# Five edits to one decoder-layer kernel: two stage edges removed, the selected branch rebuilt, queries reversed early, a bank copied in mid-logits, and an output projection of seven products

## The chip, the cores and the metric

One program on one NeuronCore of a Trainium2 chip, all of it in float32. The metric is the device time of one execution in microseconds (us), lower is better; the time of the kernel before is the median of three runs.

## The reference, cut to what matters

One layer with d_model 1024: a prompt of 1024 tokens, and 8 sample sequences of 4 new tokens each (32 rows) behind a past of 8192 tokens.

```python
def layer(x_prompt, x_sample, caches, page_table, weights):
    q, k, v, gates = split(rms_norm(x, norm_attn) @ w_in)
    a = dilated_attention(q_a, k_a, v_a)               # 8 heads: (window, dilation) (128,1), (512,4), (2048,16)
    c, p = compressed_attention(q_b, mlp(blocks of 64))# 8 query heads, 2 KV heads
    s = attention over the 16 blocks with the largest p, gathered from the paged pool
    w = attention over a window of 512
    mix = concat(a, g0 * c + g1 * s + g2 * w)          # sigmoid gates; T5 bias on every logit
    x1 = x + mix @ w_out                               # (1024 + 32) x 1024 by 1024 x 1024
    u = causal_conv3(rms_norm(x1, norm_ffn) @ w_up)    # 2 x 2816 columns
    return rms_norm(x1 + (silu(u_gate) * u_value) @ w_down, ...), new cache rows
```

## The kernel before, in words

Five functions run one after the other: `front` (the combined projection and the compression MLP), `compressed_and_dilated` (stage `cd`: the compressed and dilated attention of the sample rows, the choice of blocks, and the compressed attention of the prompt), `sample_selected` (`sb`: the selected and window branches of the samples), `prompt_attention` (`pa`: 12 pairs of prompt heads, `it`, by 8 tiles of 128 queries, which gives 96 units `u`), and `ffn`. Each has a `block` of its own: one instruction list for each engine, written out by hand, with semaphores between them. At the end of a block `Mem.end` lets GpSimd clear the stage's semaphores and every engine meets at a barrier; nothing of the next stage starts before. Each stage also allots its own PSUM tensors (eight banks of 128 x 512).

In `cd` the sample keys of four dilated tiles are transposed by TensorE (L1459), copied out by ScalarE and VectorE (L1649, L1644), and multiplied (L1478) with QX, the queries placed in a zeroed tensor: GpSimd zeroes it, VectorE places eight pieces (L1791). At its end the SP queue loads the window keys (L1427), eight tables of window bias (L125, into `sample_turned`), and stores the mixed sample rows (L1434).

In `sb`, for each of 8 sequences b and 4 chunks c, GpSimd gathers 128 keys and 128 values times 16 from the pool (L142, L2033: 1.05 MB each); TensorE transposes the keys (L2139), ScalarE and VectorE copy the banks out (L2277, L2236), TensorE forms scores; VectorE adds bias and takes the maximum; ScalarE takes one exponential of a whole row of 2052 (L2294) when c is 0 for the sequence before; then the probabilities are transposed (L2160) and multiplied with the values (L2178). Copies alternate between the two engines by the number of the bank. The window branch lies inside b = 0. The merge at the end is a chain of small steps (L2372 to L2405).

In `pa` a unit's logits go through VectorE (L1155) in chunks of at most 512 keys for two heads. TensorE's iteration s does the scores of unit s, the transposes of the probabilities of unit s-2 into three banks `psT` (L1029), and their product with the values (L1049). About a third of the banks is copied out by VectorE (L1181), the others by ScalarE (L1129). VectorE's iteration does both chunks of logits(s), the maxima, and then its copies of unit s-2:

```python
for s in range(U + 4):          # VectorE
    if s < U: logits(s)         # one or two chunks, two heads each
    if 2 <= s < U + 2: copies(s - 2)
```

Before unit 0 GpSimd reverses the first pair's queries (L1079, L1080).

In `ffn` the prompt's output projection runs by `out_tile` for 8 tiles of 128 rows: two halves of 512 columns with 8 matmuls each (L2728), VectorE adds x (L3047) to give x1, ScalarE squares and sums, VectorE and ScalarE form the norm, VectorE scales (L3055) into `xn`, TensorE transposes it (L2741), and both engines copy it out. Then follow seven products for each block of the up-projection, M1 to M7 (L2773), whose operand sums GpSimd and VectorE make (L2902 to L2907, L3071).

## Time and profile before

| | |
|---|---|
| time, median of 3 runs | 2149.1 us (2148.54 to 2150.56) |
| the profiled execution | 2152.93 us, its span 2151.2 us |
| granted TensorE clock, mean | 0.981 |
| TensorE, VectorE busy | 95%, 50% of the span |
| ScalarE, GpSimd busy | 24%, 25% |

In the rows PE is TensorE's matmul, PEld its weight load, DVE is VectorE, ACT ScalarE, POOL GpSimd, SP the sync engine; a q behind the name (PEq, SPq) is its sequencer. One 128-row matmul of 512 columns in the program is recorded as two. A program of this size runs each stage about once, so a stage's gain is read off one stretch of the timeline.

### The profile page before, as it was taken

What the parts mean: (1) busy time and instruction counts of PE and PEld (TensorE: products, weight loads), DVE (VectorE), ACT (ScalarE), POOL (GpSimd) and SP (SyncE); (2) the same over time, 40 slices, a digit from 0 to 9 for tenths busy, and PEclk for the clock granted to TensorE, in tenths of its full rate; (3) what the DMA queues carried; (4) which work ended last, traced back from release to release, by engine and by line L of the source; (5) the groups of instructions that cost most, each with busy time, mean ns of one, the idle gap of its engine ahead of it and who ended that gap; (6) DMA issues with size and microseconds to landing.
All of it is one profiled execution on the core that took longest, in us unless ns stands there. A gap on an engine that the chain in (4) does not pass through costs nothing. (4 is left out here: it accounts for less than half of the span.)

```text
span 2151.2 us, 31682 instructions
## 1 busy us (share of the span) xinstructions
PE 2051.5 (95%) x12366; PEld 1339.3 (62%) x12366; DVE 1082.9 (50%) x2484; ACT 521.6 (24%) x1106; POOL 532.7 (25%) x714
## 2 busy tenths in 40 slices
PE   6999999998977997999999999999999999999998
PEld 3445466665545665666676447888888888734443
DVE  5035455411525455666776226767777765611452
ACT  4111011001323344766766111011111111000011
POOL 1444234202024551012222101222322222303110
PEclk9999999998999998999999999999999999999999
DMA  8477678643697996222251414666556622601100
GB/s 219 138 241 258 243 294 305 236 170 109 231 339 290 402 396 226 99 67 68 82 155 39 133 60 156 215 208 204 196 196 211 220 79 60 227 12 30 42 40 39
DMA packets 156393, 373.05 MB, mean 173 GB/s; under 512 B 36981, under 2 KB 95085, under 8 KB 138189
## 3 DMA queue, kind: packets, MB, share of 16 engines
q1 hardware_dynamic: 126580, 149.89, 22.2%
q0 software_dynamic: 25280, 149.44, 18.0%
q10 hardware_dynamic: 4384, 71.68, 9.5%
q8 instruction: 99, 1.62, 0.3%
q14 instruction: 50, 0.41, 0.1%
HBM read 343.68 MB, written 98.60 MB: 206 GB/s over the span
## 5 line engine op out<-in xcount | busy, mean ns | idle before, releaser
L2773 PE MATMUL ff_ps<-ff_hx,whole_aw 128*128 128x264 f32 x2464 | 550.5, 386 | 0.9 <-DVE ff_hx L3074 0.9
L2773 PEld LDWEIGHTS ff_ps<-ff_hx,whole_aw 128*128 128x128 f32 x2464 | 467.1, 190 | 80.8 <-issue 1.4
L802 DVE STREAM_TRANSPOSE whole_space<-whole_space 128x512 f32<-128x512 f32 x256 | 155.3, 674 | 153.7 <-PE in_psH L611 142.0
L575 PE MATMUL in_ps<-in_w,in_xT 128*128 128x512 f32 (+1 forms) x512 | 201.5, 547 | 0.0
L1155 DVE CUSTOM_DVE_ANT_0 pa_L<-pa_psS,whole_space 128x512 f32<-128x512 f32 (+3 forms) x288 | 138.9, 532 | 46.8 <-PE pa_psS L1008 45.8
L575 PEld LDWEIGHTS in_ps<-in_w,in_xT 128*128 128x128 f32 x512 | 95.0, 190 | 94.2 <-issue 87.6
L1135 ACT ACTIVATE pa_L<-pa_L,pa_nm 128x640 f32<-128x640 f32 (+3 forms) x192 | 141.9, 741 | 32.3 <-DVE pa_nm L1165 30.5
L2799 PE MATMUL ff_ps<-ff_hx,whole_space 128*128 128x512 f32 x336 | 148.0, 593 | 0.0
L700 ACT ACTIVATE in_yout<-in_ps 128x128 f32<-128x128 f32 (+5 forms) x88 | 41.0, 479 | 378.8 <-PE in_ps L575 199.6
L3155 DVE SCALAR_TENSOR_TENSOR whole_space<-whole_space,ff_kept 128x1024 f32<-128x1024 f32 x88 | 123.3, 1401 | 3.1
L611 PE MATMUL in_psH<-whole_space 128*64 128x256 f32 (+1 forms) x1152 | 121.6, 364 | 0.0
L1008 PE MATMUL pa_psS<-whole_space,pa_qT 64*128 64x512 f32 (+3 forms) x576 | 115.3, 506 | 5.6 <-POOL pa_qT L1079 5.6
L589 PE MATMUL in_ps<-in_xT,in_w 128*128 128x352 f32 x384 | 117.6, 463 | 0.0
L2799 PEld LDWEIGHTS ff_ps<-ff_hx,whole_space 128*128 128x128 f32 x336 | 63.6, 190 | 80.6 <-issue 80.6
L2996 ACT ACTIVATE whole_space<-whole_space 128x1056 f32<-128x1056 f32 x22 | 23.8, 1084 | 368.6 <-DVE whole_space L3157 368.6
L1029 PE MATMUL pa_psT<-whole_ident,pa_L 128*128 128x128 f32 x816 | 111.9, 281 | 0.2 <-DVE pa_PT L1181 0.2
L1029 PEld LDWEIGHTS pa_psT<-whole_ident,pa_L 128*128 128x128 f32 x816 | 87.3, 141 | 39.5 <-issue 18.3
L2728 PE MATMUL ff_ps<-whole_space 128*128 128x512 f32 x256 | 111.2, 593 | 0.0
L1049 PE MATMUL pa_psO<-pa_PT,whole_space 128*64 128x128 f32 x1632 | 110.3, 279 | 0.9 <-DVE pa_tmp L1193 0.5
L1129 ACT ACTIVATE pa_PT<-pa_psT 128x512 f32<-128x512 f32 (+2 forms) x182 | 91.9, 541 | 75.9 <-PE pa_psT L1029 74.3
L611 PEld LDWEIGHTS in_psH<-whole_space 128*64 128x64 f32 x1152 | 74.9, 137 | 47.1 <-issue 13.0
L589 PEld LDWEIGHTS in_ps<-in_xT,in_w 128*128 128x128 f32 x384 | 71.8, 190 | 42.2 <-issue 3.8
(411 smaller groups left out, 2579.9 us busy)
## 6 DMA issues: line engine op xcount, KB each, us to landing
out_new_a_k_s<-in_cache_a_k ACTq DMA_DIRECT2D x8, 4088.0 KB
out_new_a_v_s<-in_cache_a_v ACTq DMA_DIRECT2D x8, 4088.0 KB
whole_aw<-in_w_up SPq DMA_DIRECT2D x44, 512.0 KB
in_w<-in_w_in SPq DMA_DIRECT2D x5, 2048.0 KB
whole_space<-in_cache_a_k SPq DMA_DIRECT2D x8, 1024.0 KB
whole_space<-in_cache_a_v SPq DMA_DIRECT2D x8, 1024.0 KB
ff_hx<-in_w_down SPq DMA_DIRECT2D x14, 512.0 KB, 4.7
whole_space<-in_x_prompt SPq DMA_DIRECT2D x13, 512.0 KB, 4.0
```

The lines of the kernel that those rows point to most:

```text
L575: mm = pe.matmul(ps[0:n, b, 0:width], xT[:, k, t * P:t * P + n], w[:, at % WBUF, k, 0:width], start=(k == 0), stop=(k == KC - 1))
L589: mm = pe.matmul(ps[:, b, 0:n], w[:, at % WBUF, k, c * P:c * P + P], xT[:, k, r0:r0 + n], start=(k == 0), stop=(k == KC - 1))
L611: mm = pe.matmul(psH[dh * HD:dh * HD + HD, r % 2, o0:o0 + n], w1[:, kv, t16, dh, :], rows[:, dh, t, :], start=(t16 == 0), stop=(t16 == 15) ...
L802: last = dve.transpose(put[:, dh, :, k * HD:k * HD + HD].rearrange("p t (g b) -> p t g b", g=2), got[:, :, :, dh, :])
L1008: pe.matmul(psS[:, c % 2, h, 0:w], qT[r, i, qt * P:qt * P + P], kT[i][r, j0 * P + k0:j0 * P + k0 + w], start=True, stop=True).then_inc(s_q ...
L1029: mm = pe.transpose(psT[:, b % 3, (x - x0) * P:(x - x0) * P + P], turned, ident[:, :])
L1135: nc.scalar.activation(x, x, ACT.Exp, bias=nm[:, s, h:h + 1], scale=1.0, accum_out=sm[:, s, h:h + 1]).then_inc(s_ex, 1)
L1155: dve.tensor_tensor_reduce(L[:, u % 3, h, 512 * x:512 * x + n], psS[:, c % 2, h, 0:n], T[it % 2][:, h, SEQ - w + 512 * x:SEQ - w + 512 * x ...
L2728: mm = pe.matmul(ps[:, j % 6, :], mixT[:, k, t * P:t * P + P], wo[:, k, half * 512:half * 512 + 512], start=(k == 0), stop=(k == KC - 1))
L2773: mm = pe.matmul(ps[:, bank_of(x, j, g), 0:H2], aw[:, j % 2, at, k, :], hx[:, bt, k, g * H2:g * H2 + H2], start=(k == 0), stop=(k == KH - 1))
L2799: mm = pe.matmul(ps[:, b, :], a[:, k, :], wd(k0 + k)[:, c0:c0 + 512], start=(k == 0), stop=(k == KD - 1))
L3155: dve.scalar_tensor_tensor(out=out[:, 0:SEQ], in0=U[:, v, k:k + SEQ], scalar=tap(k), in1=out[:, 0:SEQ], op0=ALU.mult, op1=ALU.add)
```

## The change

**Edges.** `front` and `cd` now share one block and one tensor of eight banks, and so do `sb` and `pa` (`Mem(..., within)` takes over the other's semaphores and ends nothing). Waits on `ended[...]`, the counts at which `front`'s engines are done, take the barrier's place, and `s_merged`, `s_mixc`, `s_q0`, `s_qr` do between `sb` and `pa`. GpSimd instead of VectorE places QX. **The end of `cd`.** The window bias goes to ScalarE's queue, the window keys and values are loaded with four neighbouring rows to a partition, the stores of mixc come after them and are waited for later. **The selected branch.** `by_act` names who copies which bank; the window branch comes one chunk later; the exponential is split in four, two at c = 0 and two at c = 1, and the sums are joined by one reduction. **First queries.** GpSimd reverses them at the end of `sb`, ahead of the merge. **Bank copy.** `copy_bank` stands between the two chunks of logits. **Seven products.** The output projection is one level of Strassen-Winograd: quadrants of 4 x 128 rows by 4 x 128 columns, seven products o1 to o7 of 4 tiles with 4 matmuls.

```diff
@@ class Mem
-    def __init__(self, nc, stack, stage):
-        self.nc, self.stack, self.stage, self.sems = nc, stack, stage, []
-        stack.callback(self.end)
+    def __init__(self, nc, stack, stage, within=None):
+        self.nc, self.stack, self.stage, self.sems = nc, stack, stage, within.sems if within else []
+        if within is None:
+            stack.callback(self.end)
@@ compressed_and_dilated, gpsimd
+            pool.wait_ge(*ended["copied"])
             pool.memset(QX[:, :, :, :], 0.0).then_inc(d_z, 1)
+            pool.wait_ge(d_q, 16)
+            pool.wait_ge(d_z, 1)
+            for h2 in range(2):
...
+                    pool.tensor_copy(put, got).then_inc(d_qx, 1)
@@ compressed_and_dilated, sync
+            sp.wait_ge(*ended["jobs"])
+            sp.wait_ge(*ended["copied"])
...
-             io["cache_win_k"][4 * x:4 * x + 4, :, :].rearrange("b (t p) c -> p b t c", p=P)).then_inc(pre.s_wk, 16)
+             io["cache_win_k"][4 * x:4 * x + 4, :, :].rearrange("b (p t) c -> p b t c", t=4)).then_inc(pre.s_wk, 16)
...
-            pre.load_window_bias(sp)
             pre.load_new_values(sp)
-            sp.wait_ge(s_st, 16 * QT)
@@ compressed_and_dilated, tensor
+                if n == 0 and h == 0:
+                    pe.wait_ge(*ended["half"])
...
+                        pe.wait_ge(*ended["by_act"])
+                        pe.wait_ge(*ended["by_dve"])
+                        pe.wait_ge(*ended["copied"])
                         pe.wait_ge(d_rep, 1)
                         pe.wait_ge(d_ab, 2)
                         pe.wait_ge(d_qx, 8)
@@ compressed_and_dilated, scalar
+            act.wait_ge(d_qk, 2 * NB)
+            pre.load_window_bias(act)
@@ sample_selected
+        def by_act(kind, *at):
+            if kind == "keys":
+                return at[2] == 3 if at[1] == 1 else at[2] % 2 == 0
+            if kind == "probs":
+                return at[1] in (0, 2)
+            return kind in ("window", "wprobs") and at[0] % 2 == 0
@@ sample_selected, gpsimd
+            pool.wait_ge(ops.s_q0, 16)
+            half = SEQ // 2
+            for x in range(2):
+                pool.tensor_copy(ops.q0[:, x * half:x * half + half].rearrange("p (t n) -> p t n", n=P),
+                                 backwards(ops.qL[0][:, x * half:x * half + half], half // P)).then_inc(ops.s_qr, 1)
@@ sample_selected, tensor
-                pe.wait_ge(s_ex, b + 1)
                 for c in range(NQ):
+                    pe.wait_ge(s_ex, NQ * b + c + 1)
@@ sample_selected, scalar
-                    if b >= 1 and c == 0:
+                    if b >= 1 and c in (0, 1):
                         act.wait_ge(s_nm, b)
-                        x = L[(b - 1) % 2]
-                        nc.scalar.activation(x, x, ACT.Exp, bias=nm[:, b - 1:b], scale=1.0,
-                                             accum_out=sm[:, b - 1:b]).then_inc(s_ex, 1)
+                        for i in (2 * c, 2 * c + 1):
+                            x = L[(b - 1) % 2][:, i * 512:LROW if i == 3 else i * 512 + 512]
+                            nc.scalar.activation(x, x, ACT.Exp, bias=nm[:, b - 1:b], scale=1.0,
+                                                 accum_out=sm[:, b - 1, i:i + 1]).then_inc(s_ex, 1)
@@ prompt_attention, vector: logits(u), behind the first chunk
+                    if x == 0 and between(u):
+                        copy_bank(u - 2, first_bank(u - 2))
...
+            def copy_bank(u, b):
...
+                if u >= 3:
+                    dve.wait_ge(s_wt, u - 2)
+                dve.wait_ge(s_tr, b + 1)
+                dve.tensor_copy(PT[:, u % 3, x0:x0 + w], psT[:, b % 3, 0:w]).then_inc(s_cd, 1)
@@ ffn, tensor
-            def out_tile(i):
...
+            def out_product(b, a, c):
+                for k in range(KH):
+                    mm = pe.matmul(ps[:, b % 6, :], a[:, k, :], c[:, k, :], start=(k == 0), stop=(k == KH - 1))
+                return mm
...
+                pe.wait_ge(s_ot2, 1)
+                for t in range(4):
...
+                    out_product(18 + t, A21o[t], T12o).then_inc(s_o6, 1)
+                    if t:
+                        transposes(t - 1)
+                pe.wait_ge(s_ot4, 1)
+                for t in range(4):
...
+                    out_product(22 + 2 * t, A22o[t], T4o).then_inc(s_o4, 1)
...
+                    pe.wait_ge(s_os3, t + 1)
+                    out_product(23 + 2 * t, A21o[t], T3o).then_inc(s_o7, 1)
+                    transposes(3 + t)
@@ ffn, gpsimd: the sums of the left operand, and the lower half's V
+            for t in range(4):
+                pool.tensor_tensor(A21o[t], A21o[t], A22o[t], ALU.add).then_inc(s_os1, 1)
...
+                pool.tensor_tensor(x1[5 + t][:, 0:512], x1[5 + t][:, 0:512], V[t], ALU.add).then_inc(s_bl, 1)
+                pool.tensor_tensor(x1[5 + t][:, 512:D], x1[5 + t][:, 512:D], V[t], ALU.add).then_inc(s_br, 1)
@@ ffn, vector
+                dve.tensor_tensor(V[t], ps[:, (18 + t) % 6, :], V[t], ALU.add).then_inc(s_v2, 1)
...
+                dve.tensor_tensor(x, x, V[t], ALU.add).then_inc(s_x1, 2)
+                if t == 3:
+                    dve.wait_ge(s_ot4, 1)
+                    dve.tensor_tensor(T3o, T12o, B11o, ALU.subtract).then_inc(s_ot3, 1)
```

The rows of the orders below name the line, the operation, the tensors and the output's shape; `late_bank` is the eight-bank tensor that `sb` and `pa` share. First SP's list where `cd` ends and `sb` begins, before:

```order
L1420 DMA scr_mixc<-cd_qp 128x512 x6
L1420 DMA scr_mixc<-cd_Lp 128x512 x2
L130 DMA sample_kcs<-scr_pen 128x1x1024
L1423 DMA sample_knew<-scr_s_w 32x128
L1424 DMA sample_knew<-out_new_slc_k_s 32x128
L1427 DMA whole_space<-in_cache_win_k 128x16x128 x2
L125 DMA sample_turned<-scr_tabW 16x1x516 x8
L120 DMA sample_turned<-scr_s_w 4x8x128
L120 DMA sample_turned<-out_new_slc_v_s 4x8x128
L1434 DMA scr_mixT<-cd_mixA 128x4x32
```

and SP's list at the same place after the change:

```order
L131 DMA sample_kcs<-scr_pen 128x1x1024
L1449 DMA sample_knew<-scr_s_w 32x128
L1450 DMA sample_knew<-out_new_slc_k_s 32x128
L1453 DMA whole_space<-in_cache_win_k 128x4x512 x2
L1458 DMA scr_mixc<-cd_qp 128x512 x6
L1458 DMA scr_mixc<-cd_Lp 128x512 x2
L121 DMA sample_turned<-scr_s_w 4x8x128
L121 DMA sample_turned<-out_new_slc_v_s 4x8x128
L1462 DMA scr_mixT<-cd_mixA 128x4x32
```

The eight tables (L125) are gone from this list, and the stores of mixc lie behind the window keys. Next VectorE in `pa`, a unit with two chunks of 512 keys, before (ISA is the fused add and maximum, and the read of its result):

```order
L1155 ISA pa_L,pa_mx<-pa_psS,whole_space 128x512
L1155 ISA pa_mx 128x1
L1155 ISA pa_L,pa_mx<-pa_psS,whole_space 128x512
L1155 ISA pa_mx 128x1
L1155 ISA pa_L,pa_mx<-pa_psS,whole_space 128x512
L1155 ISA pa_mx 128x1
L1155 ISA pa_L,pa_mx<-pa_psS,whole_space 128x512
L1155 ISA pa_mx 128x1
L1161 TENSOR_TENSOR pa_mm<-pa_mx 128x2
L1165 TENSOR_SCALAR pa_nm<-pa_mm 128x2
L1181 COPY pa_PT<-pa_psT 128x512
L1181 COPY pa_PT<-pa_psT 128x128
```

and the same unit on VectorE after the change:

```order
L1171 ISA pa_L,pa_mx<-late_bank,whole_space 128x512
L1171 ISA pa_mx 128x1
L1171 ISA pa_L,pa_mx<-late_bank,whole_space 128x512
L1171 ISA pa_mx 128x1
L1196 COPY pa_PT<-late_bank 128x512
L1171 ISA pa_L,pa_mx<-late_bank,whole_space 128x512
L1171 ISA pa_mx 128x1
L1171 ISA pa_L,pa_mx<-late_bank,whole_space 128x512
L1171 ISA pa_mx 128x1
L1179 TENSOR_TENSOR pa_mm<-pa_mx 128x2
L1183 TENSOR_SCALAR pa_nm<-pa_mm 128x2
L1196 COPY pa_PT<-late_bank 128x128
```

The copy of the first bank of unit u-2 has moved up by two fused operations and the two small ones; 31 units have it so. Last TensorE in the output projection, before (L2741 are the transposes of a finished tile, L2719 closes the sample rows):

```order
L2719 MATMUL ff_ps<-whole_space,ff_stack 32x512 x2
L2728 MATMUL ff_ps<-whole_space 128x512 x32
L2741 MATMUL ff_ps<-whole_ident,ff_hx 128x32 x8
L2728 MATMUL ff_ps<-whole_space 128x512 x16
L2741 MATMUL ff_ps<-whole_ident,ff_hx 128x128 x8
L2728 MATMUL ff_ps<-whole_space 128x512 x16
```

and TensorE at the same place after the change:

```order
L2805 MATMUL ff_ps<-whole_space,ff_stack 32x512 x2
L2809 MATMUL ff_ps<-whole_space 128x512 x72
L2876 MATMUL ff_ps<-whole_ident,ff_hx 128x32 x8
L2809 MATMUL ff_ps<-whole_space 128x512 x4
L2876 MATMUL ff_ps<-whole_ident,ff_hx 128x128 x8
L2809 MATMUL ff_ps<-whole_space 128x512 x4
L2876 MATMUL ff_ps<-whole_ident,ff_hx 128x128 x8
L2809 MATMUL ff_ps<-whole_space 128x512 x8
```

Before, a tile's sixteen matmuls lie between two sets of transposes; now 72 come first, then four between sets for three tiles, then eight, and the projection has 112 of them instead of 128.

## Rows read from the trace of the kernel before

**Rows 1.** Busy time and instructions of each engine, from the page's first part.
```profile
PE 2051.5 (95%) x12366; PEld 1339.3 (62%) x12366; DVE 1082.9 (50%) x2484; ACT 521.6 (24%) x1106; POOL 532.7 (25%) x714
```
**Rows 2.** TensorE's waits: waiting line, releaser, us in total, times, longest.
```profile
PE sb_psT L2139 <- ACT whole_space L2277: 14.1, 9, 4.6
PE pa_psT L1029 <- DVE pa_PT L1181: 11.8, 9, 1.4
PE sb_psT L2069 <- PEq L69: 9.4, 1, 9.4
...
PE pa_psS L1008 <- POOL pa_qT L1079: 5.6, 1, 5.6
PE cd_psT L1459 <- PEq L69: 5.4, 1, 5.4
```
**Rows 3.** Timeline from front to cd: start, duration, instructions, [idle before <-releaser].
```profile
507.93 0.54 POOL L890 DMA_DIRECT2D scr_qT<-in_yout  x1 [4.19 <-ACT in_yout L700]
...
512.58 2.89 PE L1459 MATMUL cd_psT<-whole_ident,whole_space 128*128 128x128 f32 x12 [5.44 <-PEq L69]
513.60 2.82 DVE L1791 COPY cd_QX<-sel_dq 64x32 f32<-64x32 f32 x8
523.42 1.94 PE L1478 MATMUL cd_psS<-sample_turned,cd_QX 128*32 128x512 f32 x8
...
532.25 1.06 PE L1478 MATMUL cd_psS<-sample_turned,cd_QX 128*32 128x512 f32 x8
```
**Rows 4.** Timeline where cd ends; SPq rows are DMA issues.
```profile
626.39 0.46 DVE L1808 COPY cd_mixA<-cd_psT 64x64 f32<-64x64 f32 x2 [0.75 <-PE cd_psT L1514]
626.80 6.30 SPq L125 DMA_DIRECT2D sample_turned<-scr_tabW  x8
...
634.07 0.39 SPq L1434 DMA_DIRECT2D scr_mixT<-cd_mixA  x1
```
**Rows 5.** Windows, cd's first us and two sequences of sb: engines' busy us, PEclk, DMA share, GB/s.
```profile
507.10:512.60 5.50, 0.06 (x2) 0.05 (x1) 0.02 (x1) 0.46 (x1) 0.60 (x2) 0.72 0.09 33
735.30:776.90 41.60, 37.80 (x487) 26.47 (x486) 20.17 (x44) 16.42 (x28) 25.54 (x24) 0.96 1.00 409
```
**Rows 6.** Timeline of sb: one value gather and one exponential.
```profile
690.29 0.96 POOL L2033 DMA_INDIRECT whole_space<-in_cache_slc_v,sample_idx  x1 [14.57 <-PE sb_psT L2139]
...
693.69 2.00 ACT L2294 ACTIVATE sb_work<-sb_work,sb_nm 128x2052 f32<-128x2052 f32 x1 [2.12 <-DVE sb_nm L2337]
```
**Rows 7.** Timeline from sb's last step to pa's first logits.
```profile
831.76 0.60 DVE L2405 TENSOR_TENSOR whole_space<-sample_mixB,sb_o 64x128 f32<-64x128 f32 x2
...
836.98 0.29 DVE L1155 CUSTOM_DVE_ANT_0 pa_L<-pa_psS,whole_space 128x128 f32<-128x128 f32 x1 [4.62 <-PE pa_psS L1008]
```
**Rows 8.** Timeline of one unit of pa with two chunks.
```profile
885.77 1.53 PE L1029 MATMUL pa_psT<-whole_ident,pa_L 128*128 128x128 f32 x12
...
886.38 0.69 DVE L1155 CUSTOM_DVE_ANT_0 pa_L<-pa_psS,whole_space 128x512 f32<-128x512 f32 x1
...
888.00 0.69 DVE L1181 COPY pa_PT<-pa_psT 128x512 f32<-128x512 f32 x1
...
888.74 0.33 PE L1029 MATMUL pa_psT<-whole_ident,pa_rgB 128*128 128x128 f32 x1 [1.44 <-DVE pa_PT L1181]
```
**Rows 9.** The output projection: group of its matmuls (busy us, mean ns), and its window.
```profile
L2728 PE MATMUL ff_ps<-whole_space 128*128 128x512 f32 x256 | 111.2, 593 | 0.0
```
```profile
1191.90:1314.20 122.30, 121.69 (x345) 58.76 (x345) 31.35 (x53) 17.84 (x39) 10.35 (x9) 1.00 0.23 78
```
**Rows 10.** Timeline of VectorE and GpSimd around one output tile, and at the end.
```profile
1248.78 0.69 DVE L3047 TENSOR_TENSOR ff_hx<-ff_ps,whole_space 128x512 f32<-128x512 f32 x1 [6.08 <-PE ff_ps L2728]
...
1251.31 1.28 DVE L3055 SCALAR_TENSOR_TENSOR ff_hx<-ff_hx,ff_rstd,whole_space 128x1024 f32<-128x1024 f32 x1 [0.27 <-ACT ff_rstd L2968]
...
1309.75 1.93 DVE L3055 SCALAR_TENSOR_TENSOR ff_hx<-ff_hx,ff_rstd,whole_space 128x1024 f32<-128x1024 f32 x1 [0.27 <-ACT ff_rstd L2968]
1310.68 2.13 POOL L2904 TENSOR_TENSOR whole_aw<-whole_aw 128x512 f32<-128x512 f32 x1
```

More of the change, by code:

```diff
@@ L892, in _ @@
             pool.wait_ge(s_ps, 32)
-    return total
+    return total, ended
 def backwards(x, tiles=1):
@@ L1140, in _, with first_bank, between @@
             n_mm = 0
+            def first_bank(u):
+                return bank0[u] if on_dve(bank0[u]) else None
+            def between(s):
+                return 2 <= s < U and first_bank(s - 2) is not None and chunk0[s + 1] - chunk0[s] == 2
             def logits(u):
@@ L2648, in up_weights @@
                                  wup[:, v, :, j * P:j * P + P]).then_inc(s_wu[j % 2], 16)
+            for i in range(1, NTILE):
+                sp.dma_start(x1[i], x_rows(order[i])).then_inc(s_x[1 + i // 5], 16)
             sp.wait_ge(s_cv, 1)
```

432 lines of the change are left out of this document (288 added, 144 removed).

## The prediction

> **What bounds the kernel now.** I read the page's busy times first: TensorE works 95% of the span, no other engine above 50% [rows 1]. So time is won only by fewer matmuls or by closing TensorE's waits. The list of its waits names the places [rows 2]: 5.4 us behind the barrier into `cd`, 9.4 into `sb`, 5.6 for the first queries of `pa`, 11.8 in nine waits for VectorE's bank copy, and 14.1 inside `sb` for ScalarE's key copies. The timelines around each place say what would be late next. Last, the windows show where TensorE is not the limit: two sequences of `sb` take 41.60 us with 37.80 us of TensorE work, at a DMA share of 1.00 and 409 GB/s [rows 5]. In the output projection TensorE is busy 121.69 of 122.30 us [rows 9].
>
> **The change part by part.** Gains are against the profiled execution's 2152.93 us.
>
> A, the edge into `cd`. TensorE starts at 512.58 after 5.44 us of waiting, then waits again while VectorE places QX (8 copies, 2.82 us) before its bank copies; the first scores end at 523.42 + 1.94 = 525.36 [rows 3]. The granted clock was 0.72 of full in the idle stretch before [rows 5], and the first scores took 1.94 us where later ones of the same form took 1.06 [rows 3]. After the change transposes can follow at 507.1. VectorE begins with bank copies, so what is late next is GpSimd: it issues its last DMA until 508.5 [rows 3], then zeroes and places QX. Its eight placements have no row; between VectorE's 2.82 us for all and twice that, I take 2.8, which with the zeroing puts QX near 512.5. The scores then end near 514.9: a gain of 10.5 (6 if GpSimd takes double and the barrier's waits come back in part, 11.5 if QX is never waited for). The rest of `cd` follows from TensorE, and keeps the shift.
>
> B, the edge into `sb`. `cd`'s last computing step ends at 626.39 + 0.46 = 626.85, but SP issues the eight tables for 6.30 us and its last store ends at 634.07 + 0.39 = 634.46 [rows 4]; TensorE's 9.4 us of waiting [rows 2] ends at 635.7. With the tables on ScalarE, idle there, and the stores of mixc issued while SP waits anyway, SP's last issue ends near 627.4, and the barrier needs its 1.2 us more: 7.0 (5 to 8). The tables are needed only by the window branch, which is a chunk later. The cover of their landing is the first three key chunks; were it gone, their 6.3 us would stand there.
>
> C, inside `sb`. The key copies wait behind a whole-row exponential of 2.00 us [rows 6], part of the 14.1 us [rows 2]; in four pieces, no copy waits for more than about 0.5. By TensorE's waits alone up to 11 us could come back. But the window at share 1.00 [rows 5] says that in the steady part the gathers set the pace: 16 gathers of 1.05 MB in 41.60 us are 2.6 us each, TensorE's 3.8 us of slack in it are their shadow. What can be won lies where DMA was not full: GpSimd's wait of 14.57 us for the first reused value buffer at 690.29 [rows 6], in which the gathers stand still. There the exponential's 2.00 us and the row of copies behind it go early, 3.5 us by the order; the rest of the dips I put at 3.5 more. I take 7, with 3 (the first refill alone) and 11 as ends. The two window loads have four times longer pieces, and start 7 us earlier; the one wait for them is in the 3.5.
>
> D, the edge into `pa`. The merge ends at 831.76 + 0.60 = 832.36, the first logits start at 836.98 after 4.62 us [rows 7], because SP waits for the block's start, and GpSimd reverses only then (5.6 us of TensorE [rows 2]). With q0 ready, scores of unit 0 are formed during the merge, so logits follow at once: 4.6 (3.5 to 5). GpSimd's reversal, about 1 us, is ahead of the merge where its engine has nothing to do.
>
> E, the bank copy. The first bank of u-2 is transposed by about 886.3 (12 transposes in 1.53 us from 885.77, three banks), while VectorE works the first chunk until 886.38 + 0.69 = 887.07; its copy starts only at 888.00 and TensorE waits 1.44 us for it [rows 8]. In mid-logits the copy ends at 887.8, 0.9 us before, and the second chunk's end moves from 887.7 to 888.4. TensorE's next need is then that chunk's bank, 0.7 later than now, in the next iteration. It has over 2 us of products in between. Of 11.8 us I take 10.5 (8 to 11.5).
>
> F, seven products. 16 matmuls fewer, at 2 x 111.2 / 256 = 0.87 us each [rows 9], are 13.9 us. Against them: the last tiles are now bound by a chain on VectorE, add (0.69) to scaling (1.28, ending 3.8 us after the add began) to transposes and copies [rows 10], while a tile of the sixth product gives TensorE only 4 x 0.87 + 1.0 = 4.5 us. VectorE's own work a tile there is two adds, scaling, copy and the small ones, 5.2 us or more, so TensorE waits 2 to 3 us over three tiles, and 0.6 at the end; another 1 for sums of B (128 x 2048) that VectorE holds. GpSimd's 20 additions at 1.27 us are off the path except for contention: where one lay beside the scaling, they took 2.13 and 1.93 instead of 1.27 and 1.28 [rows 10]. Three such meetings on the path cost 2. So 13.9 - 4 - 2 = about 8 (5 to 10; -1 if the next paragraph's rule holds throughout).
>
> The Trainium skill, page "SBUF — State Buffer", section "SBUF: two separate sides", says that VectorE and GpSimd share a pair of ports as an exclusive lock: a VectorE operation with two SBUF inputs and a GpSimd one that reads SBUF block each other wholly. The row pair above agrees in kind (0.65 us and 0.86 us lost at one overlap). By that rule the 20 additions of 1.27 us would all stand in VectorE's way, 25 us at the very most, and the projection could gain nothing.
>
> **Sum.** 10.5 + 7.0 + 7.0 + 4.6 + 10.5 + 8.0 = 47.6 us, so 2105.3 for a profiled execution. The profiled one of before stands 3.8 us above the median of its runs, so I predict 2101.5, say 2101. By the lower ends the gain is 30.5 (2118.6), by the upper ones 57 (2092).
>
> **Rivals.**
> 1. *The gathers hold `sb`.* For it: share 1.00 and 409 GB/s over 41.60 us [rows 5]. Everything that comes earlier on TensorE then waits for DMA. Against: the 14.57 us in which GpSimd itself stood [rows 6]. Gain without C: 2101 + 7 = 2108.
> 2. *The output projection gains nothing.* VectorE's chain and GpSimd's additions take turns; the pair at 1309.75 and 1310.68 shows it once [rows 10]. Its eight lower tiles' additions each meet a scaling. Gain without F: 2109.
> 3. *The edges don't open.* The waits on `ended` and on GpSimd's QX take the barrier's place, and `sb` still starts when SP is through (8 stores of mixc, two key loads). Half of A, B and D, 11 us, is gone: 2112. For it: GpSimd's list in `cd` begins with work that VectorE did. Against: 508.5 to 512.5 is before today's restart.
> 4. *The other side: the mid-logit copy holds VectorE.* VectorE stands in 31 units at a bank that TensorE has not transposed yet, since that needs the exponential of u-2, and the second chunk, its maxima and the next exponential all come later. If it stands x us and TensorE behind it, the time is 2101 + 10.5 + 31x, above 2149.1 from x = 1.2 on; at 1.3 it is 2152. For it: VectorE's list has no slack in such a unit. Against: the bank is there 0.8 us ahead [rows 8], so the transposes would have to come 2 us later.
>
> **Chances.** The forecast 0.50; rival 1 0.13; rival 2 0.13; rival 3 0.10; two of these together, near 2117, 0.06; rival 4 0.06; something I don't see 0.02. Within 0.2% (4.3 us, about what a measurement of this kernel can tell from no change) takes nearly an exact offset: 0.02. Slower is rival 4: 0.06. Faster 0.92. The range reaches down past the upper ends by a few us, for TensorE at full clock where it idled, to 2088, and up to two rivals together with their spread, 2123.
>
> **What the changed profile would show.** A: no wait on the sequencer near 507; transposes there, first scores before 516. B: no table DMA on SP; TensorE idle under 3 us between `cd` and `sb`. C: `sb` from its first matmul to the merge 7 us shorter; GpSimd's wait near 690 shorter by 3 or more; share still 1.00 in the steady part. D: first logits within 0.5 us of the merge's last step. E: no wait of 1.4 us for VectorE's copy, and no wait of VectorE for TensorE at the new copy. F: 112 matmuls in about 114 us in place of 122.3, with waits of 1 to 3 us for VectorE in the upper tiles. I am wrong if TensorE waits in `cd` for GpSimd's QX, if `sb` keeps its length, if VectorE stands at the mid-logit copy, or if the output projection's waits on VectorE sum to over 8 us.

## The result, and the profile after

The changed kernel takes 2128.79 us (median of 6 runs, 2126.58 to 2133.57); the kernel before took 2149.83 over all of its six runs. The ratio is 0.9902, 95% interval 0.9884 to 0.992: faster by 21 us, or 1%, where 48 us were predicted, and outside the predicted range of 2088 to 2123. The profiled execution of the changed kernel is 2126.58 us, so the two traces lie 26.4 us apart (spans 2151.2 and 2124.8). Against the traces the prediction missed 21.2 us.

The ledger cuts both traces at the same marks: the end of the last step of `cd`, the first matmul of `sb`, the end of the merge, the first logits and the end of the last product of `pa`, and then the first matmul of `ffn`, of the output projection, and of the second product of the up-projection.

| stretch | before, us | after, us | gain | predicted |
|---|---|---|---|---|
| start of the program to `cd`'s last step (A) | 626.85 | 615.02 | 11.8 | 10.5 |
| `cd`'s last step to `sb` (B) | 8.88 | 5.51 | 3.4 | 7.0 |
| `sb` to the end of the merge (C) | 196.64 | 190.82 | 5.8 | 7.0 |
| merge to first logits (D) | 4.61 | 0.03 | 4.6 | 4.6 |
| first logits to last product of `pa` (E) | 343.11 | 341.46 | 1.7 | 10.5 |
| last product to `ffn` | 1.90 | 7.20 | -5.3 | 0 |
| `ffn`'s sample rows | 9.87 | 12.39 | -2.5 | 0 |
| output projection (F) | 122.41 | 115.26 | 7.2 | 8.0 |
| the rest | 836.88 | 837.11 | -0.2 | 0 |

So most of the miss in these two traces lies in two places: the bank copy, and an edge of which the prediction says nothing. Of the 26.4 us, 19.7 are less busy time of TensorE (2051.5 us before, 2031.8 after) and 6.7 are shorter waits. The matmuls that the output projection saves are 13.5 of the 19.7. Most of the rest is the granted clock: TensorE's work in `cd` took 102.3 us at a granted clock of 0.91 before and 95.9 at 1.00 after, in `sb` 170.4 at 0.93 and 167.0 at 0.96.

Here is the list of TensorE's waits after the change, with the columns of [rows 2]:

```profile
PE late_bank L1040 <- ACT pa_PT L1137: 8.4, 8, 1.1
PE late_bank L2183 <- DMA whole_space<-in_cache_slc_k,sample_idx: 8.3, 6, 1.9
PE ff_ps L2796 <- PEq L70: 7.2, 1, 7.2
PE late_bank L2183 <- DVE whole_space L2280: 6.4, 7, 3.6
PE late_bank L2113 <- PEq L70: 6.0, 1, 6.0
...
PE ff_ps L2876 <- DVE ff_hx L3275: 3.2, 4, 1.0
...
PE late_bank L2172 <- DMA whole_space<-in_cache_win_v: 2.3, 1, 2.3
```

None of the two old entries for `pa` is left. But where 11.8 us were spent waiting for VectorE's copy, 8.4 are now spent waiting for ScalarE's (L1137), and TensorE's wait at the start of `ffn` (L2796) has grown from 1.9 to 7.2 us. In `sb` the 14.1 us for ScalarE's key copies are gone, but 8.3 us for gathered keys (L2183) have come, and the 1.8 for VectorE's copies have become 6.4.

At the edge into `cd` the timeline after answers to [rows 3]:

```profile
507.11 1.04 PE L1489 MATMUL joint_bank<-whole_ident,whole_space 128*128 128x128 f32 x8
...
509.72 1.38 POOL L1389 COPY cd_QX<-sel_dq 64x32 f32<-64x32 f32 x8 [0.15 <-POOL cd_QX L1381]
...
513.50 1.06 PE L1511 MATMUL joint_bank<-sample_turned,cd_QX 128*32 128x512 f32 x8
```

The transposes follow without a gap; GpSimd places QX in 1.38 us, half of VectorE's 2.82; the scores run at the warm pace of 1.06 us and end at 514.56, 10.8 us before [rows 3].

### The profile page after: what moved, and what is told of

Same layout as the page of the kernel before. It is cut to its first block and busy times, and to the rows that moved or that the text cites. A ratio compares the mean times of both kernels' runs of the same rounds, so it can differ in the third digit from the quotient of the medians.

```text
span 2124.8 us, 31736 instructions
## 1 busy us (share of the span) xinstructions
PE 2031.8 (96%) x12334; PEld 1327.2 (62%) x12334; DVE 1111.5 (52%) x2518; ACT 524.8 (25%) x1146; POOL 574.1 (27%) x746
## 2 busy tenths in 40 slices
DMA packets 156392, 373.04 MB, mean 176 GB/s; under 512 B 36981, under 2 KB 95085, under 8 KB 138189
## 5 line engine op out<-in xcount | busy, mean ns | idle before, releaser
L585 PE MATMUL joint_bank<-in_w,in_xT 128*128 128x512 f32 (+1 forms) x512 | 201.5, 547 | 0.0
L1171 DVE CUSTOM_DVE_ANT_0 pa_L<-late_bank,whole_space 128x512 f32<-128x512 f32 (+3 forms) x288 | 141.0, 532 | 42.5 <-PE late_bank L1019 41.6
L585 PEld LDWEIGHTS joint_bank<-in_w,in_xT 128*128 128x128 f32 x512 | 95.0, 190 | 94.2 <-issue 87.6
L621 PE MATMUL joint_bank<-whole_space 128*64 128x256 f32 (+1 forms) x1152 | 121.6, 364 | 0.0
L1040 PE MATMUL late_bank<-whole_ident,pa_L 128*128 128x128 f32 x816 | 113.2, 281 | 8.4 <-ACT pa_PT L1137 8.4
L1040 PEld LDWEIGHTS late_bank<-whole_ident,pa_L 128*128 128x128 f32 x816 | 87.5, 141 | 49.4 <-ACT pa_L L1143 17.6
L599 PE MATMUL joint_bank<-in_xT,in_w 128*128 128x352 f32 x384 | 117.6, 463 | 0.0
L1060 PE MATMUL late_bank<-pa_PT,whole_space 128*64 128x128 f32 x1632 | 110.3, 279 | 0.9 <-DVE pa_tmp L1213 0.5
L1137 ACT ACTIVATE pa_PT<-late_bank 128x512 f32<-128x512 f32 (+2 forms) x182 | 91.7, 540 | 56.4 <-PE late_bank L1040 55.0
L1019 PE MATMUL late_bank<-whole_space,pa_qT 64*128 64x512 f32 (+3 forms) x528 | 104.0, 498 | 0.0
L2809 PE MATMUL ff_ps<-whole_space 128*128 128x512 f32 x224 | 97.7, 593 | 1.7 <-issue 1.7
## 6 DMA issues: line engine op xcount, KB each, us to landing
in_w<-in_w_in SPq DMA_DIRECT2D x5, 2048.0 KB, 14.1
```

What stands on the lines that cost most here:

```text
L585: mm = pe.matmul(ps[0:n, b, 0:width], xT[:, k, t * P:t * P + n], w[:, at % WBUF, k, 0:width], start=(k == 0), stop=(k == KC - 1))
L599: mm = pe.matmul(ps[:, b, 0:n], w[:, at % WBUF, k, c * P:c * P + P], xT[:, k, r0:r0 + n], start=(k == 0), stop=(k == KC - 1))
L621: mm = pe.matmul(psH[dh * HD:dh * HD + HD, r % 2, o0:o0 + n], w1[:, kv, t16, dh, :], rows[:, dh, t, :], start=(t16 == 0), stop=(t16 == 15) ...
L1040: mm = pe.transpose(psT[:, b % 3, (x - x0) * P:(x - x0) * P + P], turned, ident[:, :])
L1060: mm = pe.matmul(psO[h * HD:h * HD + HD, u % 2, 0:P], V[i][:, j0 + j, v0:v0 + HD], PT[:, u % 3, (2 * j + h) * P:(2 * j + h) * P + P], star ...
L1171: dve.tensor_tensor_reduce(L[:, u % 3, h, 512 * x:512 * x + n], psS[:, c % 2, h, 0:n], T[it % 2][:, h, SEQ - w + 512 * x:SEQ - w + 512 * x ...
```

## The experiments

Ratios are to the kernel before, with 95% intervals; where a run is compared with another changed one, the difference of the two ratios is taken of 2150 us. Each interval reaches 3 to 5 us to either side, so such a difference is open by about 5 us. The stretches are those of the ledger, from each run's trace. They are one execution each; how far one can be trusted shows where the same instructions ran in several kernels. `pa` repeats within 0.5 us: it takes 341.5 to 341.9 in the six kernels that have the changed kernel's `pa`.

### The last stage's start: GpSimd's drain

In the traces every block ends with a record named DRAIN on each engine, its drain, and a barrier behind the last of them. The records of GpSimd's sequencer at the end of `pa` (start us, duration us), before and after:

```
before  1180.47 0.56 POOL DRAIN     1181.36 0.13 POOL EVENT_SEMAPHORE_RANGE_CLEAR
after   1153.21 5.48 POOL DRAIN     1159.08 0.44 POOL EVENT_SEMAPHORE_RANGE_CLEAR
```

Before, GpSimd's first drain behind the last of its gathers was the one at the end of `sb`: it began at 815.23, took 12.26 us, and was over at 827.5 while the merge still ran. In the shared block that drain is gone, and the first one behind the gathers is that of `pa`'s end, where nothing hides it. One line puts a drain back where GpSimd idles:

```diff
@@ sample_selected, gpsimd, behind the reversal of the first queries
+            pool.drain()
```

> The changed kernel with one drain of GpSimd behind its reversal of the first queries, where it then idles for 14.9 us. Theory 1 (GpSimd's drain after a stretch with gathers takes long, and the change moved it from the merge, where it was hidden, to the end of the prompt attention, where it is not): the drain at the end of the prompt attention falls from 5.48 us to about 0.6, TensorE's wait into the last stage from 7.2 to about 2, and its first sample matmuls, which ran at a low granted clock behind that wait, shorten by about 2: 7 us faster than the changed kernel, near 2121. Theory 2 (the wait is the larger set of semaphores that is cleared there, 0.44 us against 0.13, and the loading of the next stage): no change, 2128.

Measured: 2122.38 us, ratio 0.9869 (0.9852 to 0.9885), 7 us below the changed kernel's 0.9902. The new drain takes 11.52 us from 794.83 and holds nobody; the one at the end of `pa` is 0.56 us again. TensorE's wait into `ffn` is 2.29 us. The windows over `ffn`'s sample rows (us, busy us and count of PE, PEld, DVE, ACT, POOL, then PEclk, DMA share, GB/s), first of the changed kernel, then of this run:

```profile
1160.03:1172.42 12.39, 12.39 (x80) 5.06 (x81) 2.05 (x4) 1.19 (x2) 4.80 (x4) 0.65 0.87 321
```
```profile
1156.34:1166.23 9.89, 9.89 (x81) 4.44 (x81) 1.96 (x4) 1.20 (x2) 4.79 (x4) 0.83 0.85 301
```

The drain and the wait are as theory 1 has them, and the clear of the semaphores is 0.3 us longer than before and no more. The same matmuls take 9.89 us in place of 12.39, at a granted clock of 0.83 in place of 0.65, which would be theory 1's third number. It is not firm. The other kernels of this section have the same stretch behind one of the same two waits:

| TensorE's wait into `ffn` | kernels | `ffn`'s sample rows, us | granted clock |
|---|---|---|---|
| 7.2 us | the changed one, three others | 12.39, 9.66, 12.64, 12.59 | 0.65, 0.85, 0.64, 0.65 |
| 2.3 us | this run, seven others | 8.24 to 11.54 | 1.00 to 0.70 |

So the drain's cost is shown for the wait, 4.9 us, which repeats in every kernel. The clock is lower behind the longer wait in most of them, and the stretch then about 2 us longer on average, but one kernel with the wait of 7.2 us runs the stretch in 9.66.

### The bank copy

```diff
@@ prompt_attention, vector: between(s)
-                return 2 <= s < U and first_bank(s - 2) is not None and chunk0[s + 1] - chunk0[s] == 2
+                return False
```

> The changed kernel with the bank copy back behind both chunks of logits, nothing else. Theory 1 (the early copy only passes the wait on: VectorE's maxima come 0.69 us later, ScalarE's exponential with them, and then TensorE waits 1.05 us for ScalarE's copy in place of 1.44 for VectorE's): eight waits of 1.4 us for VectorE come back, eight of 1.05 for ScalarE go, and the time is 2 to 3 us longer. Theory 2 (the copy gives its 10.5 us and the prompt attention lost them elsewhere, to the shared block): 10 us longer.

Measured: 2132.05 us, ratio 0.9914 (0.9899 to 0.9929), 2.6 us above the changed kernel, which the intervals alone could not tell from nothing; but `pa` takes 344.28 us against 341.46, with its 11.8 us of waiting for VectorE back and ScalarE's 8.4 gone. So the early copy alone is worth 2.6 to 2.8 us. Where the rest went is on the timeline of the changed kernel, at the unit that answers to [rows 8] and the one behind it:

```profile
862.29 0.33 PE L1040 MATMUL late_bank<-whole_ident,pa_rgB 128*128 128x128 f32 x1
...
863.68 0.17 DVE L1183 TENSOR_SCALAR pa_nm<-pa_mm 128x2 f32<-128x2 f32 x1
...
863.88 1.15 ACT L1143 ACTIVATE pa_L<-pa_L,pa_nm 128x1024 f32<-128x1024 f32 x1 [0.83 <-DVE pa_nm L1183]
...
864.21 1.53 PE L1040 MATMUL late_bank<-whole_ident,pa_L 128*128 128x128 f32 x12
...
865.03 1.14 ACT L1143 ACTIVATE pa_L<-pa_L,pa_nm 128x1024 f32<-128x1024 f32 x1
...
866.16 1.06 ACT L1137 ACTIVATE pa_PT<-late_bank 128x512 f32<-128x512 f32 x2
...
866.79 0.44 PE L1040 MATMUL late_bank<-whole_ident,pa_L 128*128 128x128 f32 x2 [1.05 <-ACT pa_PT L1137]
```

TensorE is through with the unit 1.46 us earlier than before. But VectorE's maxima (L1183) come one copy, 0.69 us, later; ScalarE stands 0.83 us for them, and its two exponentials of 1024 columns (2.28 us) come before its bank copies of the unit that TensorE is now transposing. After three banks TensorE needs the first one free, and waits for it until 866.79. The next run moves that one copy between the exponentials (with the early drain of the run above):

```diff
@@ prompt_attention, scalar: the two exponentials of unit s
                     for h in range(2):
...
+                        if h == 0 and s >= 3 and s + 1 < U and parts(s)[5] == QT:
+                            u = s - 1
+                            act.wait_ge(s_wt, u - 2)
+                            copy_out(u, banks_of(u)[0])
+                            early.add(banks_of(u)[0])
```

> The changed kernel with GpSimd's early drain, and ScalarE's first bank copy of the unit before moved between the two exponentials of 1024 columns of a full unit. Theory 1 (TensorE's eight waits of 1.05 us for ScalarE's copy are what the early bank copy turned into; the exponentials stand in front of that copy): those waits go, the prompt attention falls from 341.5 to about 333.5, near 2114 in time. Theory 2 (the pace of these units is set by VectorE and only shows at ScalarE): the wait moves on to a third place and the prompt attention stays within 2 us of 341.5.

Measured: 2114.36 us, ratio 0.9835 (0.9817 to 0.9853), 7.3 us below the run with the drain alone; `pa` takes 332.63 us. The timeline of this run at the same unit:

```profile
867.31 1.15 ACT L1150 ACTIVATE pa_L<-pa_L,pa_nm 128x1024 f32<-128x1024 f32 x1 [0.83 <-DVE pa_nm L1195]
...
867.64 1.88 PE L1040 MATMUL late_bank<-whole_ident,pa_L 128*128 128x128 f32 x14
...
868.46 0.57 ACT L1130 ACTIVATE pa_PT<-late_bank 128x512 f32<-128x512 f32 x1
...
868.93 1.14 ACT L1150 ACTIVATE pa_L<-pa_L,pa_nm 128x1024 f32<-128x1024 f32 x1
```

All 14 transposes run through. With both copies early `pa` is 10.5 us shorter than before the change (343.11). That this is the very sum that the prediction gave to VectorE's copy alone is chance: with neither copy early `pa` takes 344.28, 1.2 us more than before, for a reason that no run here shows. Whether ScalarE's order by itself would do it was tried by putting VectorE's copy back in this kernel:

> The early drain and ScalarE's copy between exponentials, but VectorE's bank copy back behind both chunks of logits. Theory 1 (two engines stand in TensorE's way one behind the other: VectorE's copy 1.44 us, and once that is gone ScalarE's 1.05; only both together free it): the waits of 1.44 us for VectorE are back, the prompt attention takes about 343, and the time is 10 us above the run with both, near 2125. Theory 2 (ScalarE's order alone is worth the 8.9 us): prompt attention near 334, near 2116.

Measured: 2125.99 us, ratio 0.9884 (0.9869 to 0.9899), 10.5 us above the run with both, `pa` 344.13 us. The first line of its list of waits:

```profile
PE late_bank L1040 <- DVE pa_PT L1208: 11.8, 9, 1.4
```

So in `pa` VectorE's early copy alone gives 2.8 us (344.28 to 341.46), ScalarE's alone 0.15 (344.28 to 344.13), and both together 11.7, to 332.63.

### The output projection

The last stage with the `ffn` of the kernel before, all else changed (the function is put back whole; only its call is shown):

```diff
@@ the whole program
-    ffn(nc, io, scr, G, space[:, KC * (ROWS + D):n], space[:, n:], mixT, wo, aw, cv, ident, s_mix, s_wo, s_cvl, s_moved)
+    ffn(nc, io, scr, G, space[:, n:], mixT, wo, aw, cv, ident, s_mix, s_wo, s_cvl, s_moved)
```

> The changed kernel with the last stage as it was, so an output projection of 128 matmuls. Theory 1 (the seven products give what their timeline shows): 7 us longer, the projection's window 122.4 us again; the wait into the stage stays at 7.2 us. Theory 2 (GpSimd's and VectorE's additions eat the gain in another place, in the first products of the up-projection): within 2 us of the changed kernel.

Measured: 2136.59 us, ratio 0.9936 (0.9921 to 0.9951), 7.3 us above the changed kernel; the projection is 122.42 us again against 115.26. Theory 1 holds. Groups of the changed kernel in that window (line, engine, form, count, busy us, mean ns):

```profile
L2809 PE MATMUL ff_ps<-whole_space 128*128 128x512 f32 x224 | 97.7, 593 | 1.7 <-issue 1.7
L2876 PE MATMUL ff_ps<-whole_ident,ff_hx 128*128 128x128 f32 x64 | 9.0, 276 | 4.6 <-DVE ff_hx L3275 3.2 <-ACT ff_hx L3127 1.5
L3053 POOL TENSOR_TENSOR whole_space<-whole_space 128x512 f32<-128x512 f32 x4 | 7.6, 1900 | 5.8 <-PE ff_ps L2809 5.8
...
L3268 DVE SCALAR_TENSOR_TENSOR ff_hx<-ff_hx,ff_rstd,whole_space 128x1024 f32<-128x1024 f32 x4 | 6.1, 1516 | 1.1 <-ACT ff_rstd L3121 1.1
...
L3046 POOL TENSOR_TENSOR whole_space<-whole_space 128x512 f32<-128x512 f32 x4 | 5.1, 1274 | 41.3 <-PE ff_ps L2809 41.3
L3235 DVE TENSOR_TENSOR ff_hx<-ff_hx,whole_space 128x512 f32<-128x512 f32 x4 | 4.7, 1165 | 0.4
...
L3208 DVE TENSOR_TENSOR ff_hx<-ff_hx,whole_space 128x512 f32<-128x512 f32 x4 | 2.8, 693 | 0.4
```

The matmuls take 97.7 us in place of 111.2. TensorE waits 4.6 us before the transposes and 1.7 us once more. GpSimd's additions take 1.27 us in their first group (L3046) and average 1.90 in the group that runs beside VectorE (L3053); VectorE's addition of two SBUF operands averages 1.17 us in one place (L3235) and 0.69 in another (L3208). This agrees in kind with the section of the Trainium skill that the prediction cites ("SBUF — State Buffer", "SBUF: two separate sides"). All of TensorE's waits here, 6.3 us, stay far from the 25 that the prediction named as the very most by that rule.

### The selected branch and its edge

The split of the exponential undone:

```diff
@@ sample_selected, scalar
-                    if b >= 1 and c in (0, 1):
...
+                    if b >= 1 and c == 0:
+                        act.wait_ge(s_nm, b)
+                        x = L[(b - 1) % 2]
+                        nc.scalar.activation(x, x, ACT.Exp, bias=nm[:, b - 1:b], scale=1.0,
+                                             accum_out=sm[:, b - 1, 0:1]).then_inc(s_ex, NQ)
```

> The changed kernel with one exponential of 2052 columns for each sequence again, in place of four pieces; everything else in the selected branch stays. Theory 1 (the gathers set the pace of the selected branch, and the split only helps until the first value buffer comes free): 1 to 3 us longer. Theory 2 (the split is what shortened the branch): 5.8 us longer, with waits of TensorE for ScalarE's key copies of 14 us as before.

Measured: 2132.98 us, ratio 0.9918 (0.9904 to 0.9932), 3.4 us above the changed kernel, between the two theories. The intervals overlap, so the time alone doesn't show a gain. The 14 us of waits for ScalarE's key copies do not come back: its trace has 6.2 us in seven waits for VectorE's copies and 9.7 us for gathered keys, like the changed kernel's. One piece of what the split buys can be named, the last sequence (3.5 us of TensorE's waiting for the exponential against 2.2). The trace also has 7.4 us of waiting for the window values; without them its `sb` takes 193.2 us to the end of the merge, and 187.3 to 190.2 in the six kernels of the table below. So the split is worth 3 to 6 us by the traces, most of it not located.

Copies alternating as before, in the kernel with the early drain and ScalarE's moved copy:

```diff
@@ sample_selected: add()
-            on_act.append(by_act(*key))
+            on_act.append(len(use) % 2 == 0 and key[0] not in ("stats", "weights"))
```

> As the best run so far (early drain and ScalarE's copy between exponentials), with the selected branch's copies alternating between ScalarE and VectorE as before the change. Theory 1 (in the steady part the gathers set the pace, so who copies matters little): within 2 us of that run. Theory 2 (the assignment is a third or more of the branch's gain): 2 to 4 us longer, TensorE's waits for copies inside the branch above 12 us.

Measured: 2117.67 us, ratio 0.9846 (0.9833 to 0.986), 2.4 us above the run with both copies early, with overlapping intervals. The waits inside `sb` are shared out otherwise, 5.6 us for ScalarE and 3.1 for VectorE, and those for gathered keys fall to 1.8. Its trace has 10.3 us of waiting for the window values against 7.2, and without these waits its `sb` takes 188.1 us against 187.3. So theory 1 fits: who copies matters by about 1 us. That a late copy here merely takes the place of a late gather is the likely reason, but the long wait for the window values lets gathers run ahead too, and no run keeps the two apart. In the steady part of the changed kernel two sequences take 40.01 us at a share of 1.01:

```profile
716.90:756.91 40.01, 36.06 (x487) 25.87 (x487) 21.43 (x47) 16.96 (x38) 25.44 (x25) 1.00 1.01 419
```

That is 1.6 us less than the 41.60 of [rows 5], at 419 GB/s for 409, with TensorE 4 us idle in both. TensorE's own work in it is 36.06 us for 37.80, at a granted clock of 1.00 for 0.96.

The edge into `sb` gave 3.4 us of 7.0. SP's row of issues in the changed kernel, behind `cd`'s last step:

```profile
610.37 4.51 SPq L1458 DMA_DIRECT2D scr_mixc<-cd_qp  x4
...
614.56 0.46 DVE L1832 COPY cd_mixA<-joint_bank 64x64 f32<-64x64 f32 x2 [0.75 <-PE joint_bank L1547]
614.93 1.11 SPq L1458 DMA_DIRECT2D scr_mixc<-cd_Lp  x2
616.08 1.37 SPq L121 DMA_DIRECT2D sample_turned<-scr_s_w  x1
617.50 0.54 SPq L121 DMA_DIRECT2D sample_turned<-out_new_slc_v_s  x1
618.08 0.88 SPq L1462 DMA_DIRECT2D scr_mixT<-cd_mixA  x1
```

The issues take 1.1 us each on average, one of the eight stores even 12.70, at a DMA share of 1.04. The kernel before had shown the same, in a row of SP that the prediction left out (it counts only the tables behind it):

```profile
616.16 10.59 SPq L1427 DMA_DIRECT2D whole_space<-in_cache_win_k  x2
```

Two other things end near SP's last issue (618.96) in the changed kernel. The window keys are issued until 591.6 and land up to 28.6 us later, near 620.2, 0.3 us ahead of `sb`'s first matmul, which needs them. And GpSimd's drain behind its first gathers, which the barrier needs, lasts from 593.77 to 616.67; before the change it lasted from 606.16 to 622.91, hidden behind SP's issues.

To see what SP's list costs, eight stores and two loads were moved to ScalarE's queue:

```diff
@@ compressed_and_dilated, sync
-            for n in range(QT):
-                half, ch = n // 4, n % 4
-                sp.wait_ge(s_o[n % 2], n // 2 + 1)
-                sp.dma_start(scr["mixc"][ch * P:ch * P + P, half * 512:half * 512 + 512], outp[n]).then_inc(s_mixc, 16)
-            sp.wait_ge(d_qk, 2 * NB)
-            pre.load_new_values(sp)
@@ compressed_and_dilated, scalar, behind load_window_bias
+            pre.load_new_values(act)
+            for n in range(QT):
+                half, ch = n // 4, n % 4
+                act.wait_ge(s_o[n % 2], n // 2 + 1)
+                act.dma_start(scr["mixc"][ch * P:ch * P + P, half * 512:half * 512 + 512], outp[n]).then_inc(s_mixc, 16)
```

> The changed kernel with GpSimd's early drain, and the eight mixc stores and two new-value loads on ScalarE's queue instead of SP's. Theory 1 (SP's list behind the full queue is what is late at the edge into the selected branch: 3.9 us from the last computing step to SP's last issue): that stretch falls from 5.5 to about 2.2 us. Theory 2 (the window keys' landing is what is late, and the DMA engines are full at a share of 1.0): the branch starts 3 us earlier but its first transposes wait that long for the window keys, and the merge ends where it did, within 1 us.

Measured: 2119.21 us, ratio 0.9858 (0.9838 to 0.9878), 2.4 us below the run with the drain alone (0.9869), intervals overlapping. SP's last issue now ends 0.4 us behind `cd`'s last step, but theory 1's number is refuted: the stretch to `sb` does not fall to 2.2 but rises to 8.06 us, and its wait has a name:

```profile
PE late_bank L2113 <- DMA whole_space<-in_cache_win_k: 8.6, 1, 8.6
```

The barrier opens only at 621.4, and neither queue holds it: SP's last issue ends at 617.5 and ScalarE's at 618.1, but GpSimd's drain, begun at 595.94, at 620.22. The window keys land at 625.2. The branch is then 185.15 us long, so that the merge ends 2.1 us earlier than in the run with the drain alone. Next the window values were also loaded in `cd`, behind their buffer's last reader. One more wait came in with it: VectorE's first logits now wait until the store of `mixT` has landed, which SP issues behind these loads.

```diff
@@ compressed_and_dilated, sync
+            sp.wait_ge(d_pv, 2)
+            for x in range(2):
+                sp.dma_start(pre.value(4 + x).rearrange("p (b t) c -> p b t c", b=4),
+                             io["cache_win_v"][4 * x:4 * x + 4, :, :].rearrange("b (p t) c -> p b t c", t=4)).then_inc(pre.s_wv, 16)
...
@@ sample_selected, sync
-            for x in range(2):
-                sp.dma_start(pre.value(4 + x).rearrange("p (b t) c -> p b t c", b=4),
...
@@ sample_selected, vector: logits(b, c), at b == 0 and c == 0
                         dve.wait_ge(ops.s_mixc, 16 * (SEQ // P))
+                        dve.wait_ge(ops.s_mixed, 16)
```

> As the run before, with the window values also loaded at the end of the stage before, when their buffer's last reader is done, instead of at the branch's start. Theory 1 (the spread of the selected branch over its executions, 188.8 to 200.6 us, is TensorE's wait for the window values, 0 to 7.4 us): that wait is gone, the branch is at the short end of its spread, and the times of the rounds lie closer together, 2 us faster than the run before. Theory 2 (the gathers set the pace whatever comes first): the wait is gone, but gathers come later by as much, no change.

Measured: 2123.8 us, ratio 0.9883 (0.9859 to 0.9907), 5 us above the run before it with intervals that still overlap, and with the widest spread of all (2119.26 to 2133.73). The wait for the window values is gone, but the keys' 7.8 us stay and a wait of TensorE of 4.5 us for VectorE comes:

```profile
PE late_bank L2153 <- DVE whole_space L2282: 4.5, 1, 4.5
```

Just before it, at 648.58, VectorE's first logits (L2381) had stood 8.30 us for the store of `mixT` (DMA scr_mixT<-cd_mixA). That is the added wait. So this run tests two things at once, and what the early loads alone are worth stays open; theory 1's 2 us faster did not come. With all edits together:

> All three together: the early drain, ScalarE's copy between exponentials, the stores and new values on ScalarE's queue, and the window values early. If the gains add up, 21 us (the change) + 7 (drain) + 8 (ScalarE's copy) + 2 to 4 (window loads) below the kernel before: near 2110. If the first theory on ScalarE's copy is wrong, near 2118.

Measured: 2117.6 us, ratio 0.9847 (0.9828 to 0.9866), 2.6 us above the kernel with the drain and ScalarE's copy alone, intervals overlapping; VectorE stands 11.2 us for the store of `mixT` here. And the window branch one chunk earlier, in the kernel with those two edits:

```diff
@@ sample_selected: the order of the banks
-                if b == 0 and c == 2:
+                if b == 0 and c == 1:
                     add("wprobs", 0)
...
@@ sample_selected, tensor (scalar and vector alike)
+                    if b == 0 and c == 1:
+                        window_probs()
                     if b == 0 and c == 2:
-                        window_probs()
-                    if b == 0 and c == 3:
                         window_values()
```

> As the best run so far, with the window branch back one key chunk earlier (its values at c = 2). Theory 1 (the window values land when the queues let them, so multiplying them earlier makes TensorE wait for them by about one chunk, 3 us, more): 1 to 3 us longer, TensorE's wait for the window values in the profile 3 us longer than the 0 to 7.4 us seen so far. Theory 2 (the wait is made up for by the gathers, which run on meanwhile): no change within 1 us.

Measured: 2114.81 us, ratio 0.9842 (0.9829 to 0.9856), 1.5 us above, not to be told apart; TensorE's wait for the window values is 5.7 us in its profile against 7.2, where theory 1 had it 3 us longer. Theory 2 fits. From `cd`'s last step to the end of the merge the profiled executions of these kernels spread from 192.1 to 204.9 us, with 0 to 10.3 us of waiting for the window values and 0 to 8.6 for the window keys. Six of these kernels have the changed kernel's instructions in this stretch, but for the early drain in three of them, and still differ:

| kernel | `cd`'s last step to `sb` (before 8.88) | `sb` to the end of the merge (before 196.64) | of it waiting for window values |
|---|---|---|---|
| the changed one | 5.51 | 190.82 | 2.3 |
| VectorE's copy back (`e2_nomid`) | 3.31 | 188.75 | 0 |
| old `ffn` (`e3_oldffn`) | 2.88 | 195.32 | 6.7 |
| early drain (`e1_drain`) | 5.63 | 189.59 | 0.8 |
| drain, both copies early (`e5_mid`) | 3.77 | 194.53 | 7.2 |
| drain, ScalarE's copy alone early (`e9_midonly`) | 3.74 | 197.53 | 7.3 |

So the gains of B and C in the ledger are one draw. Over the six, B gives 3.2 to 6.0 us, C from -0.9 to 7.9, and both together 4.2 to 13.5, on average 8.6, where 14 were predicted. Without the wait for the window values the second stretch repeats within 3 us. What makes the window loads land early or late is open.

## Why the prediction was wrong, point by point

**Bound and places.** Half right. The step "time is won only by fewer matmuls or by closing TensorE's waits" leaves out the clock: of 26.4 us between the traces 13.5 are the matmuls, 6.7 shorter waits, and 6.2 other busy time of TensorE, which fell where its granted clock rose.

**A.** Right in number: 10.8 us to the first scores for 10.5. Of these, 6.4 are waits that are gone, by the missing barrier and the copies first on VectorE, and 4.4 are TensorE's own work, which fell from 11.1 to 6.7 us as the granted clock of this stretch rose from 0.57 to 1.00. The prediction saw the slow scores (1.94 us for 1.06) but has no term for the clock. GpSimd's QX came at 511.1, earlier than the 512.5 assumed, and nobody waited for it.

**B.** 3.4 us for 7.0 in this trace, 3.2 to 6.0 in six. The step "SP's last issue ends near 627.4, and the barrier needs its 1.2 us more" failed. SP ended 3.9 us after `cd`'s last step, for 0.6 in the sum, since its issues behind the window keys are slow at a DMA share of 1.04. Two things were put at nothing without a reason: the landing of the window keys, which the first transposes need (5.2 us after `cd`'s last step), and GpSimd's drain (1.7 us after it). With SP's list emptied the barrier opened behind GpSimd's drain, and then TensorE stood for the window keys. This is a case of the first rival's kind, DMA as the limit, at another place.

**C.** 5.8 us for 7 lies in the range of 3 to 11, but that is luck of the draw: the same instructions gave -0.9 to 7.9, by how long TensorE waited for the window values. The step "the one wait for them is in the 3.5" failed: the wait for the window values was 2.7 us before and 0 to 7.3 after. GpSimd's wait for the first reused value buffer fell by 1.3 us (14.57 to 13.26), where 3 or more were named as the sign, and 3.4 of the 5.8 us are TensorE's own work at a higher granted clock. The first rival, gathers that hold `sb`, is half true: 8.3 us of TensorE's waits now name gathered keys.

**D.** Exact: 4.58 for 4.6 us.

**E.** The failed step is "TensorE's next need is then that chunk's bank ... It has over 2 us of products in between". The sum followed the second chunk's later end to the bank of scores that TensorE fills next. It did not follow the late maxima to ScalarE's list, on which two exponentials stand before the bank copies. This cost 8.8 us: `pa` is 341.46 us long with VectorE's copy moved and 332.63 once ScalarE's is moved too. The fourth rival named the first link, maxima and exponential later, but had VectorE standing at the bank; in the unit shown VectorE does not wait there.

**The end of `pa`.** No term of the sum holds it, and this is the second failed step: removing the barrier between `sb` and `pa` was priced only at that edge. The block's end carried a drain of GpSimd of 12.26 us that the merge covered; at the next block's end it took 5.48 us in the open, and with it TensorE's wait grew by 5.3 us. Another 2.5 us at the lower clock came in this trace, though not in every kernel with that wait. The early drain took the wait back to 2.3 us, and the run was 7 us faster, give or take 5.

**F.** Right: 7.2 us for 8, by matmuls of 13.5 us less and waits of 6.3 more, for 6 in the sum. The second rival is refuted.

**The median.** The profiled executions lie 26.4 us apart, the medians 21: the one of before was 3 us above its median, the one after 2 below. The sum corrected for the first and could not for the second.

## What to carry to other kernels

When a barrier is removed, list what it did besides waiting: its drain moves to the next end of a block, and it belongs where that engine idles. When an operation is moved ahead on a busy engine, follow what it delays through the instruction lists of all engines behind it, to the wait that comes second; the gain is only the distance between the first wait and the second. Here two edits that were each worth under 3 us gave 11.7 together.

## What the hardware did that was not expected

GpSimd's drain took 5.48 us at a point 357 us behind its last gather, and 0.56 us where a drain already stood between; 22.90 us at the end of `cd`, right behind its first gathers, and 12.26 and 11.52 at the end of `sb`. What it waits for so long after the last gather no run here shows. A DMA issue on SP took up to 12.70 us while the DMA engines' share was 1.04. A placement of eight 64x32 pieces took GpSimd 1.38 us and VectorE 2.82. The window loads in pieces of four rows changed no packets: 156393 before and 156392 after, with as many under 2 KB.

The fastest kernel measured is the changed one with GpSimd's early drain and ScalarE's copy between the exponentials: 2114.36 us, ratio 0.9835 (0.9817 to 0.9853).
